# The first feed-forward's token-major rows turned by 32x32 squares and through device memory instead of by TensorE

## What is computed

```python
# first_block, last lines
hf = _rmsnorm(h, norm_ffn_g[l]) @ w_ff1[l]           # 512x1024 @ 1024x4096
h = h + jnp.square(jax.nn.relu(hf)) @ w_ff2[l]       # 512x4096 @ 4096x1024
return _rmsnorm(h, norm_final_g)
# second_block starts from this
a = rmsnorm(x, norm_pre_mix)
```

## Time and profile before

| | |
|---|---|
| median of 3 runs | 1515.67 us (1513.45 to 1517.85) |
| the profiled execution: its own time | 1514.45 us |
| its span, first to last instruction | 1512.7 us |
| TensorE busy | 99% of the span, mean granted clock 0.999 |
| VectorE, ScalarE, GpSimd busy | 75%, 50%, 41% |
| first feed-forward, up chunks 0 to 7 | 857.5 to 904.7 us |
| down chunks 8 to 15, then stage CQ | 904.7 to 948.2 us, then on |

### The profile page before, as it was taken

How to read it: one execution, slowest core, us unless ns; L and a number is a source line. 1 busy time by engine, 2 the same in 40 slices (tenths; PEclk the granted TensorE clock), 3 DMA queues, 4 the chain that set the end, 5 groups by cost and what they waited for, 6 DMA issues and landing times.

```text
span 1512.7 us, 20176 instructions
## 1 busy us (share of the span) xinstructions
PE 1491.3 (99%) x6978; PEld 1230.5 (81%) x6978; DVE 1132.6 (75%) x1872; ACT 751.5 (50%) x1255; POOL 626.2 (41%) x280
## 2 busy tenths in 40 slices
PE   9999999999999999999999999999999999999998
PEld 7888888888888887888888888776778888888886
DVE  6689999997875445876777758789755887777776
ACT  6553233454562345754444245455964745445434
POOL 3454444333334432244444445341544244444451
PEclk9999999999999999999999999999999999999999
DMA  5333333255542323323333132222653333333551
GB/s 212 98 126 98 97 98 97 84 164 150 168 150 94 97 83 112 112 95 94 105 101 109 51 94 95 82 90 88 185 147 112 140 112 97 111 114 118 140 133 56
DMA packets 77026, 170.40 MB, mean 113 GB/s; under 512 B 22660, under 2 KB 39172, under 8 KB 76680
## 3 DMA queue, kind: packets, MB, share of 16 engines
q1 hardware_dynamic: 75920, 165.64, 35.0%
q10 hardware_dynamic: 1016, 3.61, 0.7%
HBM read 154.54 MB, written 14.69 MB: 112 GB/s over the span
## 4 chain that ended last, share of the span: by engine, by line
PE 84%; DVE 6%; ACT 4%; issue 3%; POOL 1%; DMA 1%; SPq 0%; ACTq 0%; DVEq 0%; POOLq 0%
PE bank L795 84%; DMA w_raw<-in_stream 1%; POOL w_lo L655 1%; ACT w_hi L1604 1%; DVE x_sq L2359 1%; DVE cq_rstd L2295 0%; ACT l_probs L2130 0%; DVE bias L2441 0%; POOL res L764 0%; ACT l_probs L2136 0%; ACT dn_first L1898 0%; ACT L2130 0%; PE bank L1214 0%; DVE cn_lo L3015 0%; ACT L2086 0%
## 5 line engine op out<-in xcount | busy, mean ns | idle before, releaser
L655 POOL TENSOR_TENSOR w_lo<-w_raw,w_hi 128x1024 fp32r<-128x1024 f32 x191 | 471.7, 2480 | 520.9 <-ACT w_hi L1604 513.1
L795 PE MATMUL bank<-a_hi,w_hi 128*128 128x512 f32 (+1 forms) x1120 | 444.7, 397 | 1.7 <-DVE a_lo L3282 1.6
L795 PE MATMUL bank<-a_hi,w_lo 128*128 128x512 f32 (+1 forms) x1120 | 431.4, 385 | 0.0
L795 PE MATMUL bank<-a_lo,w_hi 128*128 128x512 f32 (+1 forms) x1120 | 431.1, 385 | 0.0
L1604 ACT CAST w_hi<-w_raw 128x1024 fp32r<-128x1024 f32 x199 | 204.6, 1046 | 176.2 <-DMA w_raw<-in_stream 175.9
L795 PEld LDWEIGHTS bank<-a_hi,w_hi 128*128 128x128 f32 x1120 | 210.5, 188 | 48.3 <-issue 3.9
L795 PEld LDWEIGHTS bank<-a_lo,w_hi 128*128 128x128 f32 x1120 | 210.6, 188 | 45.7 <-issue 3.4
L795 PEld LDWEIGHTS bank<-a_hi,w_lo 128*128 128x128 f32 x1120 | 210.4, 188 | 42.4
L667 POOL TENSOR_TENSOR dn_rest<-dn_raw,dn_second 128x1024 fp32r<-128x1024 f32 x39 | 93.7, 2431 | 248.3 <-DVE dn_rest L2734 248.3
L795 PE MATMUL bank<-dn_rest,f_hi 128*128 128x512 f32 x364 | 141.7, 389 | 0.0
L1898 ACT CAST dn_first<-dn_raw 128x1024 fp32r<-128x1024 f32 x54 | 55.6, 1049 | 157.8 <-DVE dn_raw L2715 157.8
(11 more groups left out here) (428 smaller groups left out, 2768.6 us busy)
## 6 DMA issues: line engine op xcount, KB each, us to landing
w_raw<-in_stream SPq DMA_DIRECT2D x199, 512.0 KB, 3.5
dn_raw<-in_stream SPq DMA_DIRECT2D x56, 512.0 KB, 3.5
p_parts<-d_parts SPq DMA_DIRECT2D x8, 640.0 KB, 3.7
d_turned<-p_parts SPq DMA_DIRECT2D x32, 160.0 KB, 3.4
l_turned<-p_parts SPq DMA_DIRECT2D x32, 160.0 KB, 3.1
p_parts<-l_parts SPq DMA_DIRECT2D x8, 384.0 KB, 3.4
res<-in_xT ACTq DMA_DIRECT2D x1, 2048.0 KB, 10.2
p_parts<-l_parts SPq DMA_DIRECT2D x8, 256.0 KB, 2.4
```

The lines of the kernel that those rows point to most:

```text
L655: nc.gpsimd.tensor_tensor(w_lo[:, j, :], w_raw[:, j, :], w_hi[:, j, :].bitcast(F32), ALU.subtract).then_inc(w_lo_done, 1)
L795: return nc.tensor.matmul(o, l, r, start=start, stop=stop)
```

## The change

The 32 transposes of TensorE and `add_turned` go. In their place:
- `norm_squares` (VectorE, i = 0): `r2` is transposed in squares of 32x32, and four copies of 32x4 gather from it `r2_col`, the scale of each token as a column.
- `y_turn(tb)` (VectorE, i = 1 to 4, after the eviction and ahead of `b_lo`): 128 tokens of `ytok` are multiplied by their column (128x1024), then transposed in squares by two operations of 128x512 into `y_squares`.
- `y_out(tb)` (SyncE): `y_squares` of the block goes to `y_parts` in device memory, 512 KB in pieces of 128 floats. `y_back(tb)`: four transfers of 128 KB bring it back in pieces of 32 floats, into `y_feature`, where it is feature-major. They stand in SyncE's queue between the loads of chunks 5 to 10 of this stage.
- `y_add(b)` (VectorE): the eight blocks are added to `res`, four in i = 7 ahead of `b_lo`, two each in i = 8 and i = 9 ahead of the addition of the bank. The first waits for all sixteen returning transfers.

```diff
+Y_TURN_AT = {1: 0, 2: 1, 3: 2, 4: 3}
+Y_ADD_AT = {7: (0, 1, 2, 3), 8: (4, 5), 9: (6, 7)}
...
# SyncE
-            for c in range(CH["FF1"] + UPS[0] + 4, CH["OA"] + 5):
+
+            def y_out(tb):
+                sp.wait_ge(sems["dn_evac"], y_turned_at(tb))
+                if tb > 0:
+                    sp.wait_ge(sems["y_stored"], 16 * tb)
+                sp.dma_start(y_parts[tb].rearrange("b p n -> p b n"),
+                             y_squares[:, tb, :].rearrange("p (b n) -> p b n", b=KB)).then_inc(sems["y_stored"], 16)
+
+            def y_back(tb):
+                sp.wait_ge(sems["y_stored"], 16 * (tb + 1))
+                for q in range(RING):
+                    r = slice(PART * q, PART * q + PART)
+                    sp.dma_start(y_feature[r, tb, :, :].rearrange("i b (a j) -> i (b a) j", j=PART),
+                                 y_parts[tb].rearrange("b (a i) n -> i (b a) n", i=PART)[:, :, r]
+                                 ).then_inc(sems["y_landed"], 16)
+
+            last_ups = CH["FF1"] + UPS[0]
+            for c in range(last_ups + 4, last_ups + 6):
+                ring(c)
+            for tb in range(TB):
+                y_out(tb)
+                if tb > 0:
+                    y_back(tb - 1)
+                ring(last_ups + 6 + tb)
+            y_back(TB - 1)
+            for c in range(last_ups + 6 + TB, CH["OA"] + 5):
                 ring(c)
...
# TensorE
-            def turn_block(i):
...
                 for j in range(KB):
                     ff_up(0, UPS[0] + j)
-                    if 2 <= j < 6:
-                        turn_block(2 * j - 4)
-                        turn_block(2 * j - 3)
...
# VectorE
+            def norm_squares():
+                dve.wait_ge(sems["dn_evac"], evac_before(0, HALVES[0]) + WHOLE_STEPS + 1)
+                V.transpose(y_part[:, :].rearrange("p (c i) -> p c i", i=PART),
+                            r2[:, :].rearrange("p (c i) -> p c i", i=PART)).then_inc(sems["dn_evac"], 1)
+                dve.wait_ge(sems["dn_evac"], evac_before(0, HALVES[0]) + WHOLE_STEPS + 2)
+                for a in range(RING):
+                    r = slice(PART * a, PART * a + PART)
+                    m = V.tensor_copy(r2_col[r, :], y_part[r, PART * a:T:P])
+                m.then_inc(sems["dn_evac"], 1)
+
+            def y_turn(tb):
+                dve.wait_ge(sems["dn_evac"], y_turned_at(tb) - 2)
+                V.tensor_scalar(ytok[:, tb, :], ytok[:, tb, :], r2_col[:, tb:tb + 1], None, ALU.mult
+                                ).then_inc(sems["dn_evac"], 1)
+                dve.wait_ge(sems["dn_evac"], y_turned_at(tb) - 1)
+                for h in range(2):
+                    d = slice(h * T, h * T + T)
+                    m = V.transpose(y_squares[:, tb, d].rearrange("p (c i) -> p c i", i=PART),
+                                    ytok[:, tb, d].rearrange("p (c i) -> p c i", i=PART))
+                m.then_inc(sems["dn_evac"], 1)
+
+            def y_add(b):
+                if b == 0:
+                    dve.wait_ge(sems["y_landed"], 16 * RING * TB)
+                V.tensor_tensor(res[:, b, :].rearrange("p (t n) -> p t n", t=TB),
+                                res[:, b, :].rearrange("p (t n) -> p t n", t=TB), y_feature[:, :, b, :], ALU.add
+                                ).then_inc(sems["dn_evac"], 1)
...
-                        if i >= 3 and i < 7:
-                            add_turned(2 * i - 6)
+                        if i == 0:
+                            norm_squares()
+                        if i in Y_TURN_AT:
+                            y_turn(Y_TURN_AT[i])
+                        for b in Y_ADD_AT.get(i, ()):
+                            y_add(b)
                         dve.wait_ge(sems["b_cast"], b_before(0, HALVES[0]) + i + 1)
                         V.tensor_tensor(b_lo[:, i, :], ff_f[:, i % 2, :], b_hi[:, i, :].bitcast(F32), ALU.subtract
                                         ).then_inc(sems["b_ready"], 1)
-                        if i >= 3 and i < 7:
-                            add_turned(2 * i - 5)
                     else:
-                        if i == KB:
-                            dve.wait_ge(sems["dn_evac"], added_at(KB - 1))
+                        for b in Y_ADD_AT.get(i, ()):
+                            y_add(b)
+                        dve.wait_ge(sems["dn_evac"], added_at(i - KB))
```

More of the change, by code:

```diff
@@ L62, with y_turned_at @@
 WHOLE_STEPS = 7
+COLUMN_STEPS = 3
+Y_TURN_AT = {1: 0, 2: 1, 3: 2, 4: 3}
+Y_ADD_AT = {7: (0, 1, 2, 3), 8: (4, 5), 9: (6, 7)}
 def done_before(s, g):
-    return (PARTS_DONE * HALVES[0] + KB) * s + PARTS_DONE * g
+    return PARTS_DONE * (HALVES[0] * s + g)
 def evac_before(s, g):
-    return (PARTS_DONE * HALVES[0] + WHOLE_STEPS + 1 + 2 * KB) * s + PARTS_DONE * g
+    return (PARTS_DONE * HALVES[0] + WHOLE_STEPS + COLUMN_STEPS + 2 * TB + KB) * s + PARTS_DONE * g
+def y_turned_at(tb):
+    return evac_before(0, HALVES[0]) + WHOLE_STEPS + COLUMN_STEPS + 2 * (tb + 1)
 def added_at(i):
-    return evac_before(0, HALVES[0]) + WHOLE_STEPS + 1 + 2 * (i + 1)
+    return y_turned_at(TB - 1) + i + 1
 def act_max(s, j):
@@ L341, in program @@
         ytok = at("ytok", [P, TB, D], BIAS0)
+        y_squares = at("y_squares", [P, TB, D], C0)
+        y_feature = at("y_feature", [P, TB, KB, P], C0 + 16384)
         def t1_of(p):
@@ L401, in program @@
         p_parts = nc.dram_tensor("p_parts", [HEADS + MLA_HEADS, P, RING * TRIANGLE * PART], F32, kind="Internal").ap()
+        y_parts = nc.dram_tensor("y_parts", [TB, KB, P, P], F32, kind="Internal").ap()
         r_parts = nc.dram_tensor("r_parts", [KB, P, T], F32, kind="Internal").ap()
@@ L1205, in ff_down @@
                 product(s, g, M3, O2, (6, 7))
-            def turn_block(i):
-                if i == 0:
-                    pe.wait_ge(sems["dn_evac"], evac_before(0, HALVES[0]) + WHOLE_STEPS)
-                if i >= RING:
-                    pe.wait_ge(sems["dn_evac"], added_at(i - RING))
-                for tb in range(TB):
-                    m = nc.tensor.transpose(ps[4 + i % RING][:, tb * P:(tb + 1) * P],
-                                            ytok[:, tb, i * P:(i + 1) * P], ident)
-                m.then_inc(sems["dn_done"], 1)
             def ff_last():
@@ L2859, in ff_whole @@
                     V.tensor_tensor(r2[:, :], rstd[:, :], rstd[:, :], ALU.mult).then_inc(sems["dn_evac"], 1)
-            def add_turned(i):
-                bank = ps[4 + i % RING][:, :]
-                dve.wait_ge(sems["dn_done"], done_before(0, HALVES[0]) + i + 1)
-                if i == 0:
-                    dve.wait_ge(sems["dn_evac"], evac_before(0, HALVES[0]) + WHOLE_STEPS + 1)
-                else:
-                    dve.wait_ge(sems["dn_evac"], added_at(i - 1))
-                V.tensor_tensor(y_part[:, :], bank, r2[:, :], ALU.mult).then_inc(sems["dn_evac"], 1)
-                dve.wait_ge(sems["dn_evac"], added_at(i) - 1)
-                V.tensor_tensor(res[:, i, :], res[:, i, :], y_part[:, :], ALU.add).then_inc(sems["dn_evac"], 1)
+            def norm_squares():
[7 more added lines that the diff above has]
+                m.then_inc(sems["dn_evac"], 1)
```

2 lines of the change are left out of this document (1 added, 1 removed).

## The result

The changed kernel takes 1525.28 us (median of 6 runs, 1524.85 to 1526.19), the kernel before beside it 1516.11 (6 runs): a ratio of 1.0063, 95% interval 1.0053 to 1.0073. The loss is clear of the noise. The time is 5.5 us above the forecast of 1519.8, inside the range and near its top. The profiled execution took 1526.19 us, its span 1524.4, against a span of 1512.7 before. So the two profiled executions differ by 11.7 us and the medians by 9.2. What follows counts in the profiled ones.

A forecast was written before the change was run, and what follows sets the result against it. TensorE, busy 99% of the span, was taken as the bound; -3.6 (turns) + 6.9 (chunk 8 stall) + 0.9 (down chunks) = +4.2 us on 1514.45, 1518.6, and 1519.8 as a median; range 1512.5 to 1526.

The forecast's parts named there:

- rival 2: TensorE's clock falls to 1.2 of 2.4 GHz in the chunk 8 stall, costing 3 us more: +7.2, 1522.8 us; chance 0.18.
- The turns, -3.6: TensorE, up chunks: four periods with turns each get 0.89 us shorter once the turns go, 3.6 us in all.
- VectorE in i = 0 to 4, nothing: norm_squares and y_turn on VectorE in the up chunks fit its idle time or later room, adding nothing to the sum.
- The queue, 6.7 us a round: SyncE's queue: load 1.5, write 1.5, four returns 3.7 us make 6.7 against a 5.44 us period; load 10 lands at 908.6.
- What is late next, 6.9 us: Chunk 8: late load 10 delays rounding, square, b_hi and b_lo 7 to 912.8, needed at 905.9; TensorE stands 6.9 us.
- The low end of the sum: Lower bound of the whole sum, -0.2 us, with the chunk 8 stall at about 2.5.
- The down chunks, +0.9 (0 to 4): Four y_add take 2.4 us on VectorE, its idle absorbs 1.5, and stage CQ sees 0.9; bounds 0 and 4.
- Rival 1: Transfers keep up, load 10 lands before 902: -2.4 us, 1513.3 us; decides from a round of 5.5 us; chance 0.22.
- Rival 3: VectorE becomes the bound in the down chunks, late adds pushing operations into GpSimd's time: +0.7, 1516.4 us; chance 0.10.
- Rival 4: The change does more than it says, a gain above 3.6 us; no chance listed.
- signs of being wrong: Those loads land within 5 us of issue; VectorE's wait for y_feature ends last; or the granted clock leaves 1.0.
- the signs that were to show the forecast: Up periods 5.44; returns over 4.7 us, loads over 3.5; late roundings 9, 10; about 7 us b_lo wait; longer a_lo wait.

The follow-up runs named there:

- e12: Kernel before, turns kept, plus the changed kernel's 20 transfers at the same queue places, carrying unused data: 1519.32 us, ratio 1.0030.
- e2: Changed kernel without its 20 transfers, y_add reading y_squares instead of y_feature, all VectorE work kept: 1515.05 us, ratio 0.9994 to the kernel before.
- e1: Kernel before with the turns taken out and nothing in their place, so part of the output is missing: 1511.29 us, ratio 0.9976.
- e3: Changed kernel with the four y_add of i = 7 behind b_lo 7 instead of ahead: 1525.79 us, ratio 1.0069 to the kernel before.
- e9: As e2 (no transfers), with the eight y_add behind b_lo of i = 5, 6 and 7: 1511.75 us, ratio 0.9982 to the kernel before.
- e7: Changed kernel with 40 extra unread matmuls filling TensorE's two gaps in chunk 8: 1523.57 us, ratio 1.0056 to the kernel before.
- e11: Changed kernel with wide pieces, loads moved ahead, load 10 before the last four returns, all eight y_add behind b_lo 7: 1516.71 us, ratio 1.0011.
- e8: Changed kernel with wide pieces, loads 6 to 9 moved ahead in SyncE's queue, y_add behind b_lo in i = 6 and 7: 1515.95 us, ratio 1.0009.

## Why the prediction came out as it did

**Direction and mechanism: right.** The round of the queue is longer than a period, ScalarE waits for loads 9 and 10 with the squares behind it, `b_lo` 7 is late, and TensorE waits in chunk 8. All four were forecast, and e12 and e2 show that the transfers cause it. The size was not right: the sum had +4.2, and +9.2 was measured. The likeliest case alone was to span 1516 to 1524, and 1525.28 lies above that; the time is inside the stated range only because the range took in rival 2 as well. Two errors of the same sign made it so: the waits are 3.1 us longer than forecast, and the clock, which the sum left out, fell. And more chance was given to a change within 0.3% (0.52) than to the loss above it that came (0.42).

**The turns, -3.6: right.** e1 gives -3.6 by the ratio, -3.9 by `a_lo` and -4.8 by the medians.

**VectorE in i = 0 to 4, nothing: right.** The scaling takes 0.74 us (0.8 taken), two transposes advance by 1.30, and the four copies of `norm_squares` take 0.68 (0.4 taken). In i = 1 the row of the scaling is 2.73 us long and ends at 875.37, 0.56 us after GpSimd's remainder (872.41 + 2.40 = 874.81): that fits a hold until the remainder's end, as forecast, counted in its duration by the trace. The transposes end at 876.7 against 877.2.

**The queue, 6.7 us a round: mis-sized.** It takes 7.7 to 7.9, and e12's is as long. The write in pieces of 512 bytes is not the cause, though it had the farthest row: with the loads it moves at 326 to 339 GB/s, where 342 was taken, so load and write together take 3.2 us (3.0 taken). The term that failed is "the returns 5.2 - 1.5 = 3.7 us", which I called priced by an identical transfer. 7.8 - 3.2 leaves 4.6 us for them, above their high bound of 3.9. Load 10, forecast to land at 908.6, is rounded at 910.02; load 9, by the same list 903.4, at 905.49.

**What is late next, 6.9 us: the step that failed.** I followed only load 10 to its end. "The four `y_add` run from 907 to 909.4, before it" did not hold, since load 9, late as well, held square 6, `b_lo` 6 (909.50) and the eviction of block 7 in front of them; they began at 910.03, behind the point from which they were meant to be hidden, and met two remainders of GpSimd. The forecast weighed that meeting for `b_lo` alone. `b_lo` 7 ended at 917.4 and not at 912.8. The waits are 10.0 instead of 6.9. That the additions alone are not the whole of it, e3 shows: behind `b_lo` they cost the same time, in the down chunks.

**The low end of the sum.** -3.6 + 2.5 + 0 is -1.1, not -0.2: the recorded sum took 0.9 for the down chunks there, and not their lower bound of 0. Nothing hangs on it.

**The down chunks, +0.9 (0 to 4): near the high end when seen alone.** e2 against e1 gives 2.7 (3.4 by `a_lo`), e9 against e1 0.9. In the kernel after it is hidden by the stall: its wait for `a_lo` is 0.5 as in the earlier trace rows.

**Rival 2, the clock: it happened too.** I had it as another case beside the forecast; it is a part of the same one, since every forecast with a stall of several us had to carry it. The pitch of the matmuls loses 3.5 us (3 taken); e7 suggests that 1 to 2 of it reach the end.

**Rival 1** (transfers in time) is refuted by the round of 7.8 us. **Rival 3** (VectorE the bound) did not set this time; in e2, e3 and e11, where the waits of chunk 8 are shorter or gone, it does. **Rival 4** had nothing for it.

**Signs named.** Two of the three signs of being wrong came, one of them in part. The granted clock left 1.0: it is 0.50 from 912 to 922. And of the two loads that were to take over 5 us from their issue, load 9 did (900.09 to 905.49), but load 10 was rounded 4.5 us after it (905.47 to 910.02): it was late because it was issued late. VectorE did not wait for `y_feature`. So by its own words the forecast, as a single case, was wrong in assuming the full clock. Of the signs that were to show the forecast: loads over 3.5 us to land: 5.2. Returns over 4.7: no, 3.7; the delay shows in the issues instead, which hold SyncE's queue for 6.6 us. Longer wait for the last `a_lo`: no, as above.

**What stays open.** The split of the 9.2 us between waits, clock and VectorE's row isn't additive: each shortened wait (e3, e7) gave back only part. Why the returns take 4.6 us here, where 3.7 was worked out from a mix of a load and four returns alone, is not shown. e12 has the same round and loses only 4.5 us: its `b_lo` are needed 3.6 us later, and no additions stand ahead of them. How much each of the two does was not taken apart. e9 shows what would be left (-2.7 us) if the rows came back in time for i = 5; no queue order was found that does it, and e8 and e11 fail for different waits.

## What to carry to other kernels

Before work is moved from the bounding engine into transfers, write down the round of the DMA queue and compare it with the period of the loads that share it, and price each kind of piece by its own rate. Here the smallest pieces, whose rate came from a lighter mix, were the term that was too low; the large ones held their rate. Then follow every late load, not only the last, through each in-order queue: what stands behind its first consumer is late too, and what is meant to be hidden may start late. Put a price on the clock wherever a stall of some microseconds is forecast; and where a shortened wait doesn't shorten the time, look which engine is saturated behind it.

## What the runs showed of the hardware

- The granted clock fell after shorter pauses than I had looked for. In the kernel after, the first matmul behind the wait of 3.69 us already ran at half, and it stayed there until 923.2, some 6 us after the work had begun again at 917.47. In e12 a pause of 2.69 us (892.9 to 896.2 with a few turns around it), and in e8 one of 2.7 us, were followed by windows of 0.79 and 0.72. Even e11's pause of 2.10 us, ending at 936.72, was followed by eight matmuls of 0.56 to 0.63 us. After the two shorter pauses without turns the first five (e8) and six (e11) matmuls still ran at nearly full pace, and the slow ones began 1.3 us (e8, 909.46) and 1.5 us (e11, 938.26) after the work had begun again. The Trainium skill's rule that the prediction named (TensorE: Matmul & The Clock Gate, "Why this matters for your kernels") agrees for the kernel after; the pauses of e8, e11 and e12 are shorter than the one it warns of.
- An operation of VectorE with one input and no PSUM (the scaling of 128x1024) took 2.73 us beside a remainder of GpSimd and 0.74 without. Transposes in squares, 1.30 for two, kept their time.
- Additions of two SBUF inputs take 0.6 us each alone; four took 6.79 and 6.78 us when two remainders of GpSimd fell among them, and eight took 7.09 us with one in between (906.62 to 909.39).
- In the kernel after, with the DMA engines busy (share 0.84 to 1.19) on loads in rows of 4 KB, writes in pieces of 512 bytes and returns in pieces of 128 bytes from one queue, stretches of loads and writes moved 326 to 339 GB/s and stretches of returns alone 130 to 187.
